# Expert gate-and-up products with 512 moved columns, a quarter of each low part subtracted on GpSimd

## What is computed

```
def swiglu(t, w_gu, w_down):
    g, u = jnp.split(t @ w_gu, 2, axis=-1)
    return (jax.nn.silu(g) * u) @ w_down
...
    for e in range(N_EXPERTS):
        y = y + combine[:, e:e + 1] * swiglu(t, w_gu[e], w_down[e])
```

## Time and profile before

| | |
|---|---|
| median of 3 runs | 1509.53 us (1508.76 to 1515.17) |
| the profiled execution, its own time | 1514.51 us |
| its span in the trace | 1512.7 us |
| PE busy | 1323.6 us, 88% |
| DVE busy | 824.6 us, 55% |
| ACT busy | 696.3 us, 46% |
| POOL busy | 104.5 us, 7% |
| HBM traffic | 271.39 MB read, 10.49 MB written |

### The profile page before, as it was taken

The page is one execution under the profiler, slowest core; times in us unless marked ns, Lnnn a source line. Parts: engine busy times, 40 slices in busy tenths (PEclk is TensorE's granted clock), DMA queues, the critical chain, the costliest instruction groups (busy, mean ns, idle before and its releaser), DMA issues.

```text
span 1512.7 us, 21813 instructions
## 1 busy us (share of the span) xinstructions
PE 1323.6 (88%) x7984; PEld 1073.4 (71%) x7984; DVE 824.6 (55%) x1252; ACT 696.3 (46%) x1067; POOL 104.5 (7%) x93
## 2 busy tenths in 40 slices
PE   4799978689899999999989957785999999999993
PEld 1576655357688888888869824473998998899883
DVE  0412376773433332333343584753888988898882
ACT  2522342263522311223253442452777777777771
POOL 4000010001111100111200010020000000000000
PEclk9899988799999999999989969897999999999997
DMA  9365513201132322223113447144899999999992
GB/s 346 117 237 209 209 69 140 84 1 56 56 101 96 132 75 70 101 100 134 70 32 122 167 148 284 57 185 153 309 323 364 378 339 344 360 371 327 355 359 98
DMA packets 74623, 282.78 MB, mean 187 GB/s; under 512 B 8576, under 2 KB 10016, under 8 KB 74432
## 3 DMA queue, kind: packets, MB, share of 16 engines
q1 hardware_dynamic: 68832, 262.17, 47.7%
q0 software_dynamic: 3568, 12.19, 2.2%
q10 hardware_dynamic: 2160, 7.55, 1.3%
HBM read 271.39 MB, written 10.49 MB: 186 GB/s over the span
## 4 chain that ended last, share of the span: by engine, by line
PE 74%; DVE 10%; DMA 7%; ACT 6%; issue 3%; ACTq 0%; POOL 0%; POOLq 0%; SPq 0%; DVEq 0%
PE ps L603 12%; PE ps L604 12%; PE ps L605 12%; PE ps L968 5%; PE ps L970 4%; PE ps L969 4%; DMA raw<-in_w_mod 3%; PE ps L983 3%; PE ps L987 3%; PE ps L985 3%; PE ps L580 3%; DVE wlo L497 2%; ACT whi L492 2%; DMA raw<-in_w_fm 1%; PE ps L838 1%
## 5 line engine op out<-in xcount | busy, mean ns | idle before, releaser
L497 DVE TENSOR_TENSOR wlo<-raw,whi 128x1024 fp32r<-128x1024 f32 (+2 forms) x367 | 480.6, 1318 | 333.3 <-ACT whi L492 326.0
L492 ACT ACTIVATE whi<-raw 128x1024 fp32r<-128x1024 f32 (+2 forms) x367 | 411.0, 1124 | 325.3 <-PE ps L605 149.5
L603 PE MATMUL ps<-hhi,whi 128*128 128x512 f32 (+1 forms) x736 | 278.5, 378 | 23.8 <-DVE hlo L1522 22.6
L604 PE MATMUL ps<-hlo,whi 128*128 128x512 f32 (+1 forms) x736 | 274.9, 374 | 0.0
L605 PE MATMUL ps<-hhi,wlo 128*128 128x512 f32 (+1 forms) x736 | 274.8, 373 | 0.0
L968 PE MATMUL ps<-whi,hs_hi 128*128 128x256 f32 x704 | 204.8, 291 | 10.7 <-DVE wlo L497 8.2
L970 PE MATMUL ps<-whi,hs_lo 128*128 128x256 f32 x704 | 197.5, 281 | 0.0
L969 PE MATMUL ps<-wlo,hs_hi 128*128 128x256 f32 x704 | 197.2, 280 | 0.0
L603 PEld LDWEIGHTS ps<-hhi,whi 128*128 128x128 f32 x736 | 140.3, 191 | 60.1 <-issue 30.5
L604 PEld LDWEIGHTS ps<-hlo,whi 128*128 128x128 f32 x736 | 140.5, 191 | 26.2
L605 PEld LDWEIGHTS ps<-hhi,wlo 128*128 128x128 f32 x736 | 140.0, 190 | 26.8
(11 more groups left out here) (265 smaller groups left out, 1651.7 us busy)
## 6 DMA issues: line engine op xcount, KB each, us to landing
raw<-in_w_gu SPq DMA_DIRECT2D x230, 512.0 KB, 5.0
raw<-in_w_dn SPq DMA_DIRECT2D x80, 704.0 KB, 8.3
raw<-in_w_mod SPq DMA_DIRECT2D x96, 512.0 KB, 4.8
raw<-in_w_fm SPq DMA_DIRECT2D x32, 512.0 KB, 3.5
raw<-in_w_out SPq DMA_DIRECT2D x16, 512.0 KB, 4.3
raw<-in_w_tg SPq DMA_DIRECT2D x8, 512.0 KB, 3.5
y_rows<-back POOLq DMA_DIRECT2D x1, 4096.0 KB, 18.7
y_rows<-ys ACTq DMA_DIRECT2D x8, 512.0 KB, 6.6
```

Of the source, the lines that this page charges most:

```text
L492: nc.scalar.activation(whi[:, v % H, 0:cols], src[:, 0:cols], ACT.Copy).then_inc(hi_ready, 1)
L497: nc.vector.tensor_tensor(wlo[:, v % H, 0:cols], landed_in(v)[0][:, 0:cols], whi[:, v % H, 0:cols].bitcast(F32), ALU.subtract).then_inc(lo ...
L603: nc.tensor.matmul(outp, whs, xh, start=first, stop=False)
L604: nc.tensor.matmul(outp, whs, xl, start=False, stop=False)
```

## The change

A group of two tiles (`FG` = 6 groups, the last with one tile) takes the place of a tile. Its units are cut anew: a unit now holds two of the eight k-slices for both tiles, where it held four k-slices of one tile. One matmul then moves 2 x 256 = 512 columns, which lie in two stretches of 256 in the slot, and a unit is 6 matmuls. The two last units, of the group with one tile, stay as they were. The host's layout stays too, so each of the first 20 units is brought by a transfer that takes 512 columns (2 KB) of each partition from two places in HBM, where it took 1024 columns (4 KB) from one.

silu, product, turn, high copy and low subtraction of the hidden columns are done once for a group, on 256 columns.

The low part of a gate-and-up unit is split: VectorE subtracts columns 0 to 767 (`LO_CUT`), GpSimd columns 768 to 1023. A new semaphore `plo_ready` counts GpSimd's part. TensorE waits for both. VectorE, before it splits a unit, waits until GpSimd has done its part of the unit before; SP, which knows only `lo_ready`, waits for one unit more than it did, and so knows that both parts of the raw buffer have been read.

```diff
+FG = 6
+LO_CUT = 768
...
+        def pool_unit(u):
+            return u + 1 if u < 2 * FJ else 2 * FJ + u - BLOCK + 1 if u >= BLOCK else None
+
+        def group_end(r):
+            return r // 4 if r < 20 and r % 4 == 3 else FG - 1 if r == 2 * FJ - 1 else None
...
+        def expert_src(base, r):
+
+            if r >= 20:
+                return d["w_gu"][1][bass.ds(base + r, 1)].rearrange("a p n -> (a p) n")
+            half, pair = r % 4 // 2, r % 2
+            four = d["w_gu"][1][bass.ds(base + r // 4 * 4, 4)].rearrange("(t h) p n -> h p t n", h=2)
+            return four[half, :, :, pair * 512:(pair + 1) * 512]
...
-                    sp.wait_ge(lo_ready, b * (NE * BLOCK) + e * BLOCK + (V_FFN[1] + r + 1))
-                    sp.dma_start(expert_ring(r)[:, 0:n], src).then_inc(expert_landed(r)[0], 16)
+                    sp.wait_ge(lo_ready, b * (NE * BLOCK) + e * BLOCK + (V_FFN[1] + r + 2))
+                    sp.dma_start(dst, src).then_inc(expert_landed(r)[0], 16)
...
+            def moved(w, s, nt, kk):
+
+                return w[:, s, 0:UNIT].rearrange("p (t k n) -> p k t n", t=nt, n=2 * P)[:, kk]
...
-                    for j in range(FJ):
-                        for half in range(2):
-                            v = v0 + 2 * j + half
+                    for g in range(FG):
+                        nt = len(tiles_of(g))
+                        wide, per = 2 * P * nt, 4 // nt
+                        o = ps[:, g % 2, 0:wide]
+                        for q in range(KT // per):
+                            v = v0 + 4 * g + q
                             pe.wait_ge(lo_ready, i * BLOCK + (v + 1))
+                            pe.wait_ge(plo_ready, i * (2 * FJ) + (v - v0 + 1))
                             s = v % H
-                            o = ps[:, j % 2, 0:2 * P]
-                            for kk in range(4):
-                                k = 4 * half + kk
-                                wh, wl = whi[:, s, kk * 2 * P:(kk + 1) * 2 * P], wlo[:, s, kk * 2 * P:(kk + 1) * 2 * P]
+                            for kk in range(per):
+                                k = per * q + kk
+                                wh, wl = moved(whi, s, nt, kk), moved(wlo, s, nt, kk)
...
                 with pool.Fori(2, n_end) as n:
-                    fetch(n)
+                    for r in range(BLOCK):
+                        u = r + H
+                        if pool_unit(u):
+                            v = V_FFN[1] + u
+                            pool.wait_ge(hi_ready, n * BLOCK + (v + 1 - 2 * BLOCK))
+                            nc.gpsimd.tensor_tensor(wlo[:, v % H, LO_CUT:UNIT], landed_in(v)[0][:, LO_CUT:UNIT],
+                                                    whi[:, v % H, LO_CUT:UNIT].bitcast(F32), ALU.subtract
+                                                    ).then_inc(plo_ready, 1)
+                        if r == 9:
+                            fetch(n)
...
-                        split_lo(dve, v0 + r + H, DUNIT if 2 * FJ <= r + H < BLOCK else UNIT, i)
+                        if pool_unit(r + H - 1):
+                            dve.wait_ge(plo_ready, i * (2 * FJ) + pool_unit(r + H - 1))
+                        split_lo(dve, v0 + r + H, DUNIT if 2 * FJ <= r + H < BLOCK else LO_CUT, i)
```

More of the change, by code:

```diff
@@ L211, in build @@
         lo_ready = sem("lo_ready")
+        plo_ready = sem("plo_ready")
         split_used = sem("split_used")
@@ L941, in rows_back, with turn_act @@
                         mm.then_inc(sum_done, 1)
[L943 to L948, removed]
+            def moved(w, s, nt, kk):
+                return w[:, s, 0:UNIT].rearrange("p (t k n) -> p k t n", t=nt, n=2 * P)[:, kk]
+            def turn_act(i, g):
+                pe.wait_ge(fh_ready[1], i * FG + (g + 1))
+                if g >= 2:
+                    pe.wait_ge(flo_ready[1], i * FG + (g - 1))
+                for n in range(len(tiles_of(g))):
+                    mm = nc.tensor.transpose(ps[:, 2 + g % 2, n * P:(n + 1) * P],
+                                             eact[:, g % 2, n * P:(n + 1) * P], ident[:, :])
+                mm.then_inc(aT_done, 1)
             def experts():
@@ L1314, in slots_hi, with act_hi @@
                                      ps[:, 6:8, :].rearrange("p b n -> p (b n)"), ACT.Copy).then_inc(hs_half, 1)
-            def act_hi(i, j):
-                act.wait_ge(aT_done, i * FJ + (j + 1))
-                nc.scalar.activation(ehi[:, j, :], ps[:, 2 + j % 2, 0:P], ACT.Copy).then_inc(fhi_ready[1], 1)
+            def act_hi(i, g):
+                act.wait_ge(aT_done, i * FG + (g + 1))
+                n = len(tiles_of(g))
+                nc.scalar.activation(ehi[:, 2 * g:2 * g + n, :].rearrange("p j n -> p (j n)"),
+                                     ps[:, 2 + g % 2, 0:n * P], ACT.Copy).then_inc(fhi_ready[1], 1)
             def experts():
@@ L1328, in experts @@
                     for r in range(BLOCK):
-                        j = r // 2
-                        if r < 2 * FJ and r % 2 == 1:
+                        g = group_end(r)
+                        if g is not None:
+                            n = len(tiles_of(g)) * P
                             act.wait_ge(split_used, i * BLOCK + (v0 + r + 1))
-                            if j >= 2:
-                                act.wait_ge(fh_ready[1], i * FJ + (j - 1))
-                            nc.scalar.activation(esg[:, j % 2, :], ps[:, j % 2, 0:P], ACT.Silu
+                            if g >= 2:
+                                act.wait_ge(fh_ready[1], i * FG + (g - 1))
+                            nc.scalar.activation(esg[:, g % 2, 0:n].rearrange("p (t n) -> p t n", n=P),
+                                                 ps[:, g % 2, 0:2 * n].rearrange("p (t n) -> p t n", n=2 * P)[:, :, 0:P],
+                                                 ACT.Silu
                                                  ).then_inc(sg_ready[1], 1)
-                            if j:
-                                act_hi(i, j - 1)
+                            if g:
+                                act_hi(i, g - 1)
                         split_hi(act, v0 + r + H, DUNIT if 2 * FJ <= r + H < BLOCK else UNIT, i)
                         if r == 2 * FJ:
-                            act_hi(i, FJ - 1)
+                            act_hi(i, FG - 1)
                         if r == 2 * FJ + 1:
```

64 lines of the change are left out of this document (38 added, 26 removed).

## The result

The changed kernel takes **1534.71 us** in the median of 4 runs (1533.27 to 1536.20), the kernel before 1512.34 us over the same runs. The ratio is **1.0139, with a 95% interval from 1.012 to 1.0157**: slower by some 21 us by the ratio (22.4 between the medians), clear of the 0.5% that a measurement of this kernel can tell. The forecast was 15.5 us slower, 1525. The direction and the place were right, the size was a quarter to a third too small. Of the 9.7 us between 1525 and 1534.7, 2.8 come from the starting point: the forecast counted from a median of 1509.5, and with the fourth run the kernel before stands at 1512.3.

A forecast was written before the change was run, and what follows sets the result against it. TensorE was taken as the bound, its feeding chain just in time. A pass: 1.85 + 0.34 - 0.25 = 1.94 us; eight passes 15.5 us, giving 1530.0 for the profiled execution and 1525.0 for the median, range 1506 to 1541.

The forecast's parts named there:

- The bound and the place: Expert stage: TensorE is the bound, fed just in time by the chain through the low subtraction, 0.02 us to spare.
- GpSimd beside VectorE: Split low subtraction: one engine waits for the other, so a unit's low part takes 1.60 us instead of 1.27.
- the whole-instruction rule: GpSimd beside VectorE: whoever issues first holds the shared pair throughout; a unit takes 1.67, some 2.5 us more in all.
- The start of a pass: Fourth unit of a pass, late already: with 1.60 for 1.27 it comes 0.34 us later.
- TensorE's own saving: Matmuls of 512 columns instead of two of 256: 120 pairs save 0.002 us each, 0.25 us a pass.
- T: The end of the last matmul record of a tile, from which the chain feeding TensorE is costed.
- The transfer in GpSimd's queue: Indirect transfer between units 12 and 13 on GpSimd, taking 1.19 us: makes unit 13 late by about 0.6 us.
- The end of a pair: Before units 6, 10, 14, 18: low part late by 0.47 us; with the indirect transfer, 1.85 us a pass.
- The signs: Profile: GpSimd subtractions above 0.9 us or VectorE's above 1.1, TensorE waits 15 us or more, pass about 53.8, no raw wait.
- That the engines don't get in each other's way: Rival 1, VectorE and GpSimd subtractions: no collision, 4.2 us less, 1505 us; chance 0.20.
- Strict turns at every unit: Rival 2, VectorE always first, then GpSimd: every unit costs 1.64 us against 1.47, 27 us, 1537; chance 0.10.
- Transfers as the limit: Rival 3, down-unit weight transfers: ScalarE waits about 1 us a pass, 8 us on top, 1533; chance 0.10.

The follow-up runs named there:

- e1: The changed kernel with VectorE subtracting all 1024 columns, GpSimd none and plo_ready gone: 1515.36 us, ratio 1.001 to the kernel before.
- e3: The changed kernel with GpSimd's subtraction replaced by a memset that writes and does not read, all waits kept: 1515.08 us, ratio 1.0004.
- e7: The changed kernel with unit 13, behind the indirect transfer on GpSimd's queue, subtracted whole by VectorE: 1533.52 us, ratio 1.0125.
- e5: The changed kernel without VectorE's wait for plo_ready, SP waiting instead until TensorE has used the unit: 1531.79 us, ratio 1.011.
- e6: The changed kernel with VectorE subtracting all, whole 4 KB units laid out on the host, and SP issuing one unit earlier: 1515.88 us, ratio 1.0016.
- e4: The changed kernel with LO_CUT = 896, so GpSimd takes 128 columns and VectorE 896: 1525.68 us, ratio 1.0076.
- e10: The changed kernel with VectorE's two pair_in operations moved from step 3 to step 26 of the pass before, where GpSimd is idle: 1535.0 us, ratio 1.0143.

## Why the prediction was right, point by point

**The bound and the place**: right. The down part did not change; all of the loss is in the units that GpSimd takes part in.

**GpSimd beside VectorE**: right, and it was the deciding step. The two take turns, with the 0.60 us after VectorE's end that the step gave. e1 and e3 show the cause from two sides: without GpSimd's subtraction, and with GpSimd writing but not reading. Of the two values weighed, 1.60 from the rows and 1.67 by the whole-instruction rule of the Trainium skill ("SBUF — State Buffer", section "Who interferes with whom"), the fourth unit of a pass bears the first out: 1.60 us from VectorE's start to TensorE's, which with the 0.04 in front of VectorE's start and without the 0.06 of TensorE's is 1.58 after the high copy. The prediction compared the two from different points, since its 1.60 holds that 0.04 and its 1.67 doesn't. From VectorE's start they are 1.56 and 1.67, and measured is 1.54.

**The start of a pass**: 0.34 us forecast. Distances from units 0 to 2 together are 5.96 against 5.58, 0.38.

**TensorE's own saving**: 0.25 us a pass forecast, and none came. The matmuls are in fact cheaper than the row of down matmuls led to expect: an unhindered unit of six takes 1.37 in e1 and e3, 0.229 for each, and not 1.40. But e1's gate-and-up part is 0.17 longer, since the step costed the end of a pair only with the collision. By its own numbers and VectorE's 1.23 alone the unit comes at T + 1.68 + 1.27 + 0.06 = T + 3.01, late by 0.14. Counted from e1, the saving was forecast 0.4 us a pass too high. How much of that stands in the changed kernel is not shown, since there the larger lateness at the same places takes its room.

**The transfer in GpSimd's queue**: 0.6 us forecast for unit 13; 2.23 against 1.50 is 0.73 (e1 has 1.47). e3 shows it with no collision at all. The terms were not those of the forecast: in the pass read above the transfer's record takes 0.95 us and not 1.19, but begins 0.82 after VectorE's subtraction of unit 12 has ended (1242.50 after 1241.68) and not 0.23. That the sum is so near is in part luck.

**The end of a pair**: this is **the step that was mis-sized**. It forecast 0.47 at units 6, 10, 14 and 18 and nothing at the others, and then took 1.85 with the transfer. Where nothing stands between, as at 18, it is 0.52 (1.96 against 1.44). At 10 it is absent, and at 6 it is spread: after minus before is 0.20 from unit 5 and 0.23 from unit 6, then 0.12 and 0.18 from units 10 and 11, 0.15 from 13, 0.11 from 15 and from 19. The sentence that failed is that the other units, with a period of 1.42 against TensorE's 1.40, only fail to win time back. They lose it, 0.1 to 0.2 at a time. Distances from 3 to 21 together are +2.47 us; the step and the saving had +1.60. The missing 0.9 us a pass are the 7 us between the forecast's rise and the measured one. What makes the other units late by these amounts was not tried unit by unit; e7 shows only that a delay taken away at one unit mostly comes back behind it.

**The signs.** Those named beforehand came: 1.13 and 1.23 us in the mean, 17.1 us of TensorE waiting for either part, and no wait of ScalarE for `raw`. The pass is 54.8 us where about 53.8 was named.

**The rivals.** That the engines don't get in each other's way was wrong. Strict turns at every unit was wrong as told: many units run in 1.47 to 1.55, and e5, without the wait that was to enforce them, saves 0.3 us a pass. Transfers as the limit was wrong: no wait of ScalarE for `raw` shows in the changed kernel, the slowest landing between 1200 and 1300 us is 8.2 us and not 9.7, and e6 gains nothing.

## What to carry to other kernels

Before you hand a part of VectorE's work to an idle GpSimd, look in the trace for one place where both read SBUF and see whether the later one is stretched by what is left of the earlier one: if so, the two lengths nearly add up, and an engine at 7% busy is no free help. A memset in place of the disputed operation, with all the semaphores of the split kept, tells a shared read path from the cost of a handshake in one run. And in this stage, where one engine is busy for 97% of a stretch, what helped was closing its single largest gap, the start of a pass, and not shortening a step that was just in time.

## What the runs showed of the hardware that was not expected

VectorE's `tensor_scalar` on 128 columns, with one tensor and one scalar column from SBUF, took 766 ns beside GpSimd's subtraction, 491 ns in e4 beside the shorter one, and 281 ns without it (e1 and e10). The forecast had reckoned with the two-operand operations alone. In e3 it took 281 ns too, but hardly any memset overlapped it. One that began within the last 0.13 us of the pair took 0.70 us instead of 0.64:

```profile
1223.73 0.48 DVE L1887 TENSOR_SCALAR pair_in<-slots,posx 128x128 f32<-128x128 f32 x2
...
1224.08 0.70 POOL L1478 MEMSET wlo<- 128x640 f32 x1 [0.47 <-ACT whi L516]
```

Whether this operation, unlike the subtraction, also excludes a write is left open; it wasn't tried by itself.

TensorE's first matmul after a wait costs more than the wait. At 1227.41 it has a record of 0.50 us where the others have 0.39, and the next starts 0.34 after it, not 0.23. Its weights are loaded only then, while those of a matmul in the stream are loaded when the one before it starts:

```profile
1227.41 0.19 PEld L1002 LDWEIGHTS ps<-whi,hs_hi 128*128 128x128 f32 x1 [1.80 <-POOL wlo L1477]
```

That the load is what lengthens it is a reading of these rows, not shown by a run. A stage that is late often by little pays this each time; I did not measure its share apart from the rest.
